# Opening of a two-block kernel on one core: tokens in halves, norm in token layout, h split tile by tile from PSUM, first three units on high slabs, bias read backwards

## What is computed

```
h = rmsnorm(x, norm_mix_g[layer])
z = h @ w_in[layer]
qa, ka, va, qb, kb, vb, ga, gb = columns of z        # 5120 columns in all
qa = apply_rope(qa, cos_a, sin_a); ka = apply_rope(ka, cos_a, sin_a)
ya = diff_attention(qa, ka, va, lam, ...)
yb = chunk_band_attention(qb, kb, vb, rel_bias)       # scores * 1/8 + rel_bias[clip(dist) + 256]
...
x = x + merged @ w_out[layer]; then cross attention, swiglu, and the whole second block
```

## Time and profile before

| | |
|---|---|
| median of 3 runs | 1798.88 us (1798.59 to 1800.63) |
| the profiled execution, its own time | 1800.05 us |
| its span, first to last instruction | 1798.2 us |
| TensorE busy | 1729.0 us, 96% of the span |
| VectorE, ScalarE, GpSimd busy | 50%, 37%, 43% |
| first matmul of the first unit | 41.01 us into the span |
| start of unit 3 of `rope` | 59.82 us |

### The profile page before, as it was taken

One profiled execution on the slowest core, in us unless ns is written; L12 is line 12 of the kernel. 1 busy time (PEld: TensorE's weight loads), 2 busy tenths in 40 slices (PEclk: granted clock), 3 DMA queues, 4 the chain that ended last, 5 costly groups with the idle time before them and its releaser, 6 DMA issues.

```text
span 1798.2 us, 20290 instructions
## 1 busy us (share of the span) xinstructions
PE 1729.0 (96%) x7986; PEld 1354.5 (75%) x7986; DVE 895.9 (50%) x1233; ACT 663.2 (37%) x1036; POOL 770.9 (43%) x338
## 2 busy tenths in 40 slices
PE   5999999999999889999999998999999899999997
PEld 4777666677986667777777787787777688888886
DVE  5626656477424543333324655364565677162624
ACT  6124434355433434444442343463232323222222
POOL 2333222245741347777775333322133344444441
PEclk9999999999999989999999999999999899999999
DMA  5232211033541235555554222412034223333331
GB/s 186 74 90 71 59 47 51 27 123 106 156 137 47 59 94 164 165 164 168 163 170 136 82 72 78 145 53 59 24 88 126 85 83 102 97 94 95 104 95 59
DMA packets 293555, 179.86 MB, mean 100 GB/s; under 512 B 7961, under 2 KB 277811, under 8 KB 293204
## 3 DMA queue, kind: packets, MB, share of 16 engines
q1 hardware_dynamic: 291132, 170.63, 32.5%
q10 hardware_dynamic: 1768, 5.81, 1.0%
q0 software_dynamic: 560, 2.12, 0.3%
HBM read 174.22 MB, written 4.32 MB: 99 GB/s over the span
## 4 chain that ended last, share of the span: by engine, by line
PE 93%; DVE 3%; ACT 2%; issue 1%; DMA 1%; ACTq 0%; POOL 0%; DVEq 0%; SPq 0%
PE ps L1062 60%; PE ps L1074 13%; PE ps L1088 6%; PE ps L1366 2%; PE ps L1228 2%; PE ps L1196 1%; PE ps L1310 1%; PE ps L1208 1%; PE ps L1291 1%; PE ps L1187 1%; PE ps L1543 1%; PE ps L1141 0%; PE ps L1509 0%; DMA tok<-in_x_dram 0%; PE ps L1385 0%
## 5 line engine op out<-in xcount | busy, mean ns | idle before, releaser
L552 POOL TENSOR_TENSOR WL<-raw,WH 128x1024 fp32r<-128x1024 f32 (+2 forms) x330 | 768.5, 2337 | 987.8 <-ACT WH L571 987.6
L571 ACT ACTIVATE WH<-raw 128x1024 fp32r<-128x1024 f32 (+2 forms) x330 | 331.4, 1007 | 812.6 <-PE ps L1062 665.0
L1062 PE MATMUL ps<-hH,WH 128*128 128x512 f32 x808 | 205.9, 397 | 0.2 <-DVE qG L2051 0.2
L1062 PE MATMUL ps<-hL,WH 128*128 128x512 f32 x808 | 199.7, 389 | 0.0
L1062 PE MATMUL ps<-hH,WL 128*128 128x512 f32 x808 | 199.6, 389 | 0.0
L1062 PEld LDWEIGHTS ps<-hH,WH 128*128 128x128 f32 x808 | 150.8, 188 | 42.1 <-issue 3.8
L1062 PEld LDWEIGHTS ps<-hL,WH 128*128 128x128 f32 x808 | 151.0, 187 | 32.4
L1062 PEld LDWEIGHTS ps<-hH,WL 128*128 128x128 f32 x808 | 151.0, 187 | 32.2
L1074 PE MATMUL ps<-hH,WH 128*128 128x512 f32 x328 | 138.0, 421 | 0.7 <-DVE vfTc L2053 0.7
L1074 PE MATMUL ps<-hL,WH 128*128 128x512 f32 x328 | 129.1, 394 | 0.0
L1074 PE MATMUL ps<-hH,WL 128*128 128x512 f32 x328 | 129.0, 393 | 0.0
(11 more groups left out here) (461 smaller groups left out, 2767.8 us busy)
## 6 DMA issues: line engine op xcount, KB each, us to landing
raw<-in_w_in_dram SPq DMA_DIRECT2D x64, 512.0 KB, 3.6
raw<-in_w_mlp_dram SPq DMA_DIRECT2D x64, 512.0 KB, 3.9
raw<-in_w_ada_dram SPq DMA_DIRECT2D x48, 512.0 KB, 3.6
raw<-in_w_gate_up_dram SPq DMA_DIRECT2D x44, 512.0 KB, 3.6
raw<-in_w_out_dram SPq DMA_DIRECT2D x16, 512.0 KB, 3.7
raw<-in_w_ckv_dram SPq DMA_DIRECT2D x16, 512.0 KB, 3.9
raw<-in_w_down_dram SPq DMA_DIRECT2D x16, 448.0 KB, 3.5
raw<-in_k_dft_dram SPq DMA_DIRECT2D x17, 256.0 KB, 2.7
```

Of the source, the lines that this page charges most:

```text
L552: pool.tensor_tensor(WL[un.slot][:, 0:s_.kt, 0:n], raw[un.slot][:, 0:s_.kt, 0:n], WH[un.slot][:, 0:s_.kt, 0:n].bitcast(F32), ALU.subtract) ...
L571: act.activation(WH[un.slot][:, 0:s_.kt, 0:n], raw[un.slot][:, 0:s_.kt, 0:n], ACT.Copy).then_inc(high_done, 1)
L1062: ins = pe.matmul(dst, w[un.slot][:, q, 0:m], a[:, q, :], start=(k == 0), stop=(k == 3 * kt - 1))
```

## The change

It rewrites the opening up to unit 3, and how the bias comes to be.

- SyncE loads `tok` in two halves of 512 features (`tok_in`, `tok2_in`), then the first three slabs, and only then the bias table, `swap`, the rope tables and the `lam` vectors. `anti` is gone. The 18 small vectors are issued by ScalarE.
- The sum of squares is taken from `tok` itself: ScalarE squares each of the four token tiles of a half with `accum_out` (`tok_square`), which gives one number for each token on its partition. VectorE finishes it on 128x4 numbers, ScalarE takes the root, and four matmuls with the identity (L1176) spread it to `bank(7)`; ScalarE copies that to `r`.
- The feature tiles stay in four PSUM banks. `hH` and `hL` are made from the bank, tile by tile, and VectorE copies the tile to `x` behind that. Tiles 0 to 3 are turned ahead of the vectors, tiles 4 to 7 between the first products.
- Units 0, 1 and 2 first take both passes on `WH` (`start_high`), column tile by column tile, and then their pass on `WL` (`start_low`). The two `swap` matmuls of units 0 and 1 follow behind unit 2.
- The bias is no longer turned: GpSimd reads it from DRAM straight into `bias_t`, behind `WL` of unit 2, and VectorE reads it with a step of -1. The scaling by 8 is done on the small table. The 32 matmuls and the eight copies go.
- ScalarE's three table changes for `silu` and `exp` move behind the `rope` slabs, and VectorE's small `lam` operations and the mask behind the `rope` stage.

```diff
             sp.dma_start(ident[:], t["k_square"][0]).then_inc(tok_in, 16)
-            sp.dma_start(tok[:], t["x"][0].rearrange("(t p) d -> p t d", p=P)).then_inc(tok_in, 16)
-            for k, dst in enumerate((swap, anti)):
-                sp.dma_start(dst[:], t["k_square"][1 + k]).then_inc(const_in, 16)
...
+            for e in range(2):
+                some = slice(e * D // 2, (e + 1) * D // 2)
+                sp.dma_start(tok[:, :, some], t["x"][0].rearrange("(t p) d -> p t d", p=P)[:, :, some]).then_inc((tok_in, tok2_in)[e], 16)
...
-            load(0, first_u("gate"))
+            load(0, SLOTS)
+            sp.dma_start(rel_ext[:, 0:REL], t["rel_bias"][0]).then_inc(rel_in, 16)
+            sp.dma_start(swap[:], t["k_square"][1]).then_inc(const_in, 16)
...
+            load(SLOTS, first_u("gate"))
```

```diff
             (GpSimd, in the loop over the units, behind WL)
+                if un.u == SLOTS - 1:
+                    pool.wait_ge(rel_ok, 1)
+                    pool.dma_start(bias_dram[:, :], rel_ext[:]).then_inc(rel_out, 16)
+                    pool.wait_ge(rel_out, 16)
+                    pool.dma_start(bias_t[:], bass.AP(bias_dram, MAX_REL - P + 1, [[1, P], [768, B_HEADS], [1, S]])).then_inc(rel_back, 16)
```

```diff
             (ScalarE)
-            prep(ST, 0, x)
+            act.wait_ge(tok_in, 32)
+            for tt in range(ST):
+                tok_square(0, tt)
             act.wait_ge(vec_ok, 1)
             for k in range(DT):
-                act.activation(hH[:, k, :], x[:, k, :], ACT.Identity, scale=vcol("norm_mix_g", k)).then_inc(mix_high, 1)
-            stat("x", r)
-            for u in range(SLOTS):
-                high(u)
-            for h in range(B_HEADS):
-                act.wait_ge(rel_mm, h + 1)
-                act.activation(bias_t[:, h, :], bank(5 + h % 2), ACT.Copy, scale=float(B_DH) ** 0.5).then_inc(bias_ok, 1)
+                act.wait_ge(x_t, k + 1)
+                act.activation(hH[:, k, :], bank(3 + k % 4), ACT.Identity, scale=vcol("norm_mix_g", k)).then_inc(mix_high, 1)
+                if k in (1, 2, 4):
+                    high((1, 2, 4).index(k))
+            act.wait_ge(tok2_in, 16)
+            for tt in range(ST):
+                tok_square(1, tt)
+            act.wait_ge(const_in, CONSTS_IN)
+            root_table()
+            act.wait_ge(stat_v, 1)
+            act.activation(tok_r[:, 0:4], tok_r[:, 0:4], ACT.Sqrt).then_inc(stat_r, 1)
+            act.wait_ge(stat_sum, 1)
+            act.activation(r[:], bank(7), ACT.Copy).then_inc(r_ok, 1)
+            follow("rope")
```

```diff
             (TensorE)
+            def token_tile(k):
+                if k >= 4:
+                    pe.wait_ge(x_c, k - 3)
+                for i in range(ST):
+                    ins = pe.transpose(ps[:, 3 + k % 4, i * P:(i + 1) * P], tok[:, i, k * P:(k + 1) * P], ident[:])
+                ins.then_inc(x_t, 1)
+            def start_high(j, c):
+                un = at["rope", j]
+                if c == 0:
+                    pe.wait_ge(high_done, un.u + 1)
+                for e, a in enumerate((hH, hL)):
+                    pe.matmul(bank(un.bank), WH[un.slot][:, c, :], a[:, c, :], start=(c == 0 and e == 0), stop=False)
+            def start_low(j):
+                un = at["rope", j]
+                pe.wait_ge(low_done, un.u + 1)
+                for c in range(DT):
+                    ins = pe.matmul(bank(un.bank), WL[un.slot][:, c, :], hH[:, c, :], start=False, stop=(c == DT - 1))
+                ins.then_inc(unit_done, 1)
...
+            pe.wait_ge(tok2_in, 16)
+            for c in range(DT + 2):
+                if c < DT:
+                    pe.wait_ge(h_ok, c + 1)
+                    start_high(0, c)
+                    start_high(1, c)
+                if c >= 2:
+                    start_high(2, c - 2)
+                if c < 4:
+                    token_tile(4 + c)
+            start_low(0)
+
+            pe.wait_ge(stat_r, 1)
+            for tt in range(ST):
+                ins = pe.matmul(ps[:, 7, tt * P:(tt + 1) * P], tok_r[:, tt:tt + 1].to_broadcast([P, P]), ident[:],
+                                start=True, stop=True, skip_group_check=True)
+            ins.then_inc(stat_sum, 1)
+            start_low(1)
+            start_low(2)
```

```diff
             (VectorE)
             for k in range(DT):
                 dve.wait_ge(mix_high, k + 1)
-                low(x[:, k, :], vcol("norm_mix_g", k), hH[:, k, :], hL[:, k, :]).then_inc(h_ok, 1)
+                low(bank(3 + k % 4), vcol("norm_mix_g", k), hH[:, k, :], hL[:, k, :]).then_inc(h_ok, 1)
+                dve.tensor_copy(x[:, k, :], bank(3 + k % 4)).then_inc(x_c, 1)
...
-                        out=pB[n % 4][:, 0:nk], in0=bank(3 + n % 3, nk), in1=bias_t[:, h, S - nk:S],
+                        out=pB[n % 4][:, 0:nk], in0=bank(3 + n % 3, nk), in1=bias_t[:, h, 0:nk][:, ::-1],
```

More of the change, by code:

```diff
@@ L480, in build @@
         block = ctx.enter_context(nc.Block())
-        CONSTS_IN = 16 * 2 + 2
+        CONSTS_IN = 16 + 2
         @block.sync
@@ L559, in _ @@
             own = Own(act, own_a)
-            act.wait_ge(const_in, CONSTS_IN)
+            for name, n in VEC_ROWS:
+                c = VEC_AT[name]
+                side, c = (0, c) if c < VEC_SPLIT else (1, c - VEC_SPLIT)
+                src = t[name]
+                while len(src.shape) > 1:
+                    src = src.rearrange("a b -> (a b)") if len(src.shape) == 2 else src.rearrange("a b c -> (a b c)")
+                act.dma_start(vecload[c:c + n, side, :], src.rearrange("(n p) -> n p", p=P)).then_inc(vec_in, 16)
             def high(u):
@@ L631, in _ @@
             act.activation(lam_s[:, 2:4], lam_s[:, 0:2], ACT.Exp).then_inc(lam_exp, 1)
-            follow("rope")
             def keep_v(dst, n0, tt=ST):
@@ L1123, in turn_final @@
                 ins.then_inc(fin_t, 1)
+            def token_tile(k):
[16 more added lines that the diff above has]
+                ins.then_inc(unit_done, 1)
             pe.wait_ge(tok_in, 32)
-            prep(tok, ST, 0)
-            pe.wait_ge(const_in, CONSTS_IN)
+            for k in range(4):
+                token_tile(k)
             pe.wait_ge(vec_in, 16 * len(VEC_ROWS))
@@ L1132, in _ @@
             pe.transpose(ps[:, 1, 0:n], vecload[0:n, 1, :], ident[0:n, 0:n]).then_inc(vec_t, 1)
[L1134 to L1143 removed]
+            pe.wait_ge(tok2_in, 16)
[16 more added lines that the diff above has]
+            start_low(2)
+            pe.wait_ge(const_in, CONSTS_IN)
             for i in range(9):
[L1146 to L1148 removed]
+                if 2 < i < 8:
                     unit(at["rope", i], hH, hL)
@@ L1648, in rest @@
                 return dve.tensor_tensor(dl, src, dh.bitcast(F32), ALU.subtract)
-            def prep(tiles, n0):
-                n = tiles * P
-                own.step(dve.memset(acc[:], 0.0))
-                for k in range(DT):
-                    dve.wait_ge(x_sq, n0 + k + 1)
-                    dve.tensor_tensor(acc[:, 0:n], acc[:, 0:n], tmp[2 + k % 2][:, 0:n], ALU.add).then_inc(x_acc, 1)
-                    dve.wait_ge(x_acc, n0 + k + 1)
             def keep_final(k):
@@ L1703, in _ @@
                     dve.wait_ge(roped, k + 1)
+            dve.wait_ge(lam_exp, 1)
+            own.step(dve.tensor_tensor(lam_s[:, 6:7], lam_s[:, 3:4], lam_s[:, 2:3], ALU.subtract))
+            own.step(dve.tensor_scalar(lam_s[:, 7:8], lam_s[:, 6:7], -LAM_INIT, None, ALU.add))
+            dve.wait_ge(rel_back, 16)
+            dve.memset(bias_t[0:CHUNK, :, 0:CHUNK], NEG * float(B_DH) ** 0.5).then_inc(bias_ok, 1)
             def times_r(dst, rr=r, n=S):
@@ L1915, in out_c @@
                     c = 2 * h + j
-                    rest(bank(b_), oH[:, c, :], oL[:, c, :]).then_inc(pv_out["c"], 1)
-                dve.wait_ge(pv_out["c"], 2 * h + 2)
+                    rest(bank(b_), oH[:, c, :], oL[:, c, :]).then_inc(pv_out, 1)
+                dve.wait_ge(pv_out, 2 * h + 2)
             each("cq", query_tile, 0, 3)
```

94 lines of the change are left out of this document (32 added, 62 removed).

## The result

The changed kernel takes 1784.28 us (median of four runs, 1783.05 to 1785.54); the kernel before took 1798.81 beside it (four runs, 1798.59 to 1800.63). The ratio is 0.9915, with a 95% interval of 0.9901 to 0.9928. That is 14.5 us less, where 20.4 were forecast. The time lies in the range, near its upper end. That end was made of late vectors and a late clock; what brought the time there is a loss behind unit 3, for which the range had no term, so that it fell inside is in part luck. The profiled execution took 1783.37, its span is 1781.6 us.

The account below looks back on a forecast made before the run. TensorE, busy 96% of the span, bounds the kernel, so only its waits can give time back; unit 3 of `rope` moves from 59.8 to 39.3, 20.5 us off the 1798.88 median, giving 1778.4 us, range 1774.0 to 1786.0.

Parts of the forecast that it names:

- late vectors: Rival in the opening: vectors land at 13.7, `hH` starts 4 us later, 1782.4 us; vectors or tokens late: 0.14.
- late clock: Rival in the opening: TensorE's clock rises 5 us later, 2.5 us lost, 1780.9; full form 1789.9; chance 0.17.
- Tokens: Opening: first half of `tok` lands at 6.5, bounds 5.4 and 9.1; 16 transposes end at about 10.1.
- Vectors: Opening: ScalarE's 18 issues end at 6.7, last landing estimated at 9.2, other bound 13.7; `vec_ok` at 11.5.
- TensorE from `WH1`: Opening: TensorE has work without a break from 15.9; high-pass matmuls and 16 transposes make 12.3 us.
- Clock: Opening: TensorE starts at 1.2 GHz and rises after 5.2 us of work, adding 2.6 us.
- `WL` passes, spreading, `swap`: Opening, units 0 to 2: `WL0` pass 1.8, spreading matmuls 0.8, two more `WL` passes 3.7, two `swap` 1.7 us.
- The root: Opening, ScalarE: the norm's root is ready at 30.6, needed at 32.6, so covered by 2.0 us.
- the rival of a held GpSimd: GpSimd stands until the 2 MB bias has landed, `WL3` comes at 49.1, 6.1 us lost, 1784.5; chance 0.05.
- The step of -1: VectorE's 32 reversed bias reads: no cost taken, within 10% of 290 to 692 ns; rival of slow reads 0.02.
- the stretch from unit 3 to the end as long as before, within 2 us: Sign expected in the changed profile: everything behind unit 3 of `rope` keeps its length within 2 us.
- nothing behind unit 3 waits on a clock of its own: Answer to the rival that gain is given back later: loads are released by `low_done`; run spread 2.0 us covers clock falls.

Follow-up runs that it names:

- e3: Changed kernel with 46 unused TensorE transposes in its idle time ahead of and behind the turned vectors; 1781.78 us, unit 3 at 38.33.
- e1: Changed kernel with one tiny ScalarE activation delaying GpSimd's `WL` at the opening of stage `out`, so VectorE's `mgL` starts first; 1780.26 us.
- e2: Kernel before the change with one tiny VectorE copy ahead of `mgL` of tile 6, so GpSimd's `WL` starts first; 1803.49 us, ratio 1.0020.
- e10: Changed kernel with `norm_mix_g` loaded and turned first, as in e7, but without the tiny ScalarE operation of e1; 1776.7 us, ratio 0.9868.
- e7: Changed kernel with `norm_mix_g` loaded and turned first, other vectors later, squares behind the `hH` tiles, plus e1's tiny ScalarE operation; 1773.65 us, ratio 0.9855.
- e0: The changed kernel as it is, run again as reference; 1783.36 us (1779.77 to 1784.76), ratio 0.9905, kernel before 1800.19.

## Why the forecast was right, and where it was not

**The opening: right in its sum (39.62 against 39.3), with two terms off that cancel.**
- *Tokens*: landing at 6.34 against 6.5. Right.
- *Vectors*: the failed term. ScalarE's 18 issues ended at 8.0, not 6.7, and TensorE's wait ended at 12.45, not 9.2. `hH` started at 13.70 instead of 12.0. (The late issues held ScalarE too: its first four squares ended at 12.3, not 11.6.) The value should have been taken near the upper bound of 13.7: the row of `swap` was a measurement, the 2.5 us behind the last issue was not, and the rule beside it leaned the same way.
- *TensorE from `WH1`*: 17.48, not 15.9. From there work runs on without a break.
- *Clock*: 1.5 us, not 2.6 (e3). It rose at 20.7, near the "about 21" of the prediction, but from a start 1.6 us later, so 3.2 us at the lower level counted and not 5.2.
- *`WL` passes, spreading, `swap`*: 1.81, 0.89, 3.66 and 1.72, against 1.8, 0.8, 3.7 and 1.7. Right.

The vectors added 1.6 us; the clock gave 1.1 back. The work of the high passes took 12.6 instead of 12.3, and the 0.5 for hand-offs was not needed. That the sum came out within 0.3 us is luck, then: four misses of both signs.

**What was to be hidden was hidden.** ScalarE, GpSimd and the reversed read in the changed kernel (the last: duration ns min/median/max, first and last start us):

```profile
30.31 0.21 ACT L635 ACTIVATE tok_r<-tok_r 128x4 f32<-128x4 f32 x1
32.69 0.94 POOL L549 DMA_DIRECT2D bias_t<-bias_ext  x1 [1.71 <-DMA bias_ext<-rel_ext]
35.91 7.53 POOL L542 TENSOR_TENSOR WL<-raw,WH 128x1024 fp32r<-128x1024 f32 x3 [2.29 <-ACT WH L573]
```

```profile
L1787 DVE CUSTOM_DVE_ANT_0 pB<-ps,bias_t x32: 292/492/693, 190.7 to 322.4; 128x128 f32<-128x128 f32 x8, 128x256 f32<-128x256 f32 x8, 128x384 f32<-128x384 f32 x8, 128x512 f32<-128x512 f32 x8
```

The root was ready at 30.5, wanted at 33.35: cover 2.8 us. GpSimd issued the read of the bias in 0.94 us and went on with `WL` at 35.91, while the transfer took 8.5 us to land: the rival of a held GpSimd is out. The step of -1 costs nothing, 292, 492 and 693 ns against 290, 492 and 692.

**The step that failed** is "the stretch from unit 3 to the end as long as before, within 2 us", and under the rivals "nothing behind unit 3 waits on a clock of its own". The stretch is longer by 3.6 us in the first profile (1742.0 against 1738.4). The tie at stage `out` takes 3.9 us at its place in every trace with the new opening that has it. That it costs 3.1 to 3.3 us of the whole time is what the medians of e1 and e2 say; e2 is clear of noise, and e10 against e7 agrees. I had asked only whether transfers would be late; I had not asked where two engines start within 0.1 us of each other, with TensorE's banks behind the loser. The rows for it were in the trace of before (409.34 and 409.39, and L1701 with its 681 to 2925 ns in the earlier trace rows, which I used for the opening alone). By the medians the sum nearly closes: with the tie mended (e1) the gain is 19.9 us of the 20.3 that the opening gives, though e1's own profile, with the first fall and later ones in it, keeps 18.3.

**What is left.** Of the 5.9 us between forecast and result the opening explains 0.3 and the tie 3.1 to 3.3. For the rest: the same two programs stood 14.5 us apart in the first runs and 16.8 in e0's, and e0 alone spreads from 1779.77 to 1784.76. Two profiles of the one program differ by 3.6 us (1783.37 and 1779.77), and two clock falls account for that (e0). That the same makes the 2 us between the medians is only argued. In the first profile alone the account is: 20.2 from the opening, 1.7 lost in the first fall, 3.9 at `out`, and about 2 back between the two and behind them, which leaves 16.6. The prediction had answered such falls with the spread of three runs of the kernel before. Its upper bound is also added up loosely: half of the later clock, 2.5, is 1.25 and not 1.6, which would put it near 1785.5; the measured 1784.28 lies within either.

## What to carry to other kernels

A shift of the whole program is not neutral for what comes later: wherever VectorE and GpSimd hold each other up, as at `out`, and start within a tenth of a microsecond, a small change upstream may turn their order. Look in the trace for pairs like the earlier trace rows's L1701, where one operation has two durations, and see who stands behind the one that loses; move what TensorE waits for ahead of it. And when the value of an unknown landing must be chosen, take it near the nearest row that was measured in the same traffic.

## What the runs showed of the hardware

- A VectorE operation with two SBUF inputs that starts 0.05 us ahead of GpSimd's takes 0.69 us; one that starts 0.08 us behind takes 2.85 (2.78 in e2, 0.13 behind). I had not expected that so small a difference far from the edit would be worth 3 us.
- The clock column can mislead at the start of a trace. It shows 1.00 for the first 16 transposes of the changed kernel, but they took 0.23 us each, twice what they take behind 20.7 (0.44 for four); the earlier trace rows have 1.00 for 24 slow bias matmuls in the same way.

```profile
6.34:10.01 3.67, 3.67 (x16) 3.27 (x16) 0.00 (x0) 1.98 (x3) 0.00 (x0) 1.00 1.07 364
```

- SyncE stood for microseconds in its issues of the first three slabs, with the tokens under way: 0.5, 2.9 and 3.6 us, where the loads issued from 10.93 on took 0.4 to 0.5 each (timeline):

```profile
2.21 7.11 SPq L498 DMA_DIRECT2D raw<-in_w_in_dram  x3
```

What was queued behind it (the bias table, `swap`) came later by that, with cover enough.
